# Block counts ahead of the gates, and twelve small matmuls on constants in four short waits of TensorE, in the routing of a mixture-of-experts step

## The chip, the cores and the metric

The kernel runs on one core of one Trainium2 chip. Its time is the device time of one execution in microseconds. It is written by hand in the Bass language: every engine (TensorE or PE, VectorE or DVE, ScalarE or ACT, GpSimd or POOL, and SyncE or SP, which issues most DMAs) has its own program, run in the order in which it is written, and the programs wait for each other on semaphores.

## The reference, cut to what matters

One layer of a decoder on 288 tokens (256 prompt positions and 8 x 4 sample positions) of width 1024, all in float32. First two token-mixing branches and a projection, then a mixture of 32 experts, of which each token uses four:

```python
logits = x2 @ w_router + b_router
top_vals, top_idx = lax.top_k(logits, TOP_K)          # 4 of 32
gates = jax.nn.softmax(top_vals, axis=-1)
...
gu = xb @ w_up[e] + b_up[e]                            # 1024 -> 2048
gate, up = jnp.minimum(gu[:, :F], 7), jnp.clip(gu[:, F:], -7, 7)
act = (up + 1.0) * (gate * jax.nn.sigmoid(1.702 * gate))
out = act @ w_down[e] + b_down[e]                      # 1024 -> 1024
y[token] += out * gate_of_that_token
```

An expert's up weights are 8 MB and its down weights 4 MB, so the 32 experts bring in 384 MB.

## The kernel before

**Stages.** The mixing branches take the first part of the span. Then comes the routing stage (about 350 to 376 us), which this change touches, and then the loop over blocks. A block is up to 32 tokens of one expert. Here 52 blocks come out of the 32 experts; an expert with more than 32 tokens has two.

**Ring of weights.** A buffer `ring` has twelve slots of 1 MB. Slots 0 to 7 hold the up weights of one expert, slots 8 to 11 its down weights. SyncE loads expert 0 while the mixing stage ends (`load_slot(0, k)`). For every further expert it loads slot k as soon as TensorE has used slot k for the last block of the expert before, which it knows from `items_before` (the index of that last block) and the counters `up_used` and `down_used`. In the kernel before, this loop over experts begins with `sp.wait_ge(items_known, 1)`, line 378.

**Routing.** TensorE computes the logits of three token tiles (line 1172 for the two prompt tiles, 1199 for the sample tile), VectorE picks the top four in `route` (lines 817 to 823), giving a 0/1 `mask`. Matmuls with triangular and all-one matrices on the mask give each token its rank within its expert (lines 1204 to 1211) and the counts of tokens of each expert (lines 1214 and 1215, semaphore `counted`). With the ranks, TensorE gathers the tokens of block 0 (`gather_prompt`, `gather_sample`, lines 997 and 1004), ScalarE copies them (`take_rows`), TensorE transposes them (`turn_rows(0)`, line 969) and VectorE scales them into `xT` (`take_x(0)`, line 695). Only then can TensorE start `up(0)` to `up(7)`, the eight up steps of block 0: eight matmul instructions each on one slot (line 1229). The rest of block 0 (its bias, activation and down steps) belongs to body 0 of the loop.

**VectorE in the routing stage, in this order:** the ranks, `take_x(0)`, the gates (exponentials times mask, sum, reciprocal, product: lines 859 to 862), `comb` (the gates at their places in the block, line 866), then the block counts: eight comparisons of the counts with 32, 64, ... (line 872), their sum (874), plus one (875), a running sum over experts in five doublings (878 and 879), and from it the list of blocks (882 to 889, semaphore `listed`), `items_before` and `n_bodies` (890, 891). TensorE turns the list into a row (line 969, semaphore `list_turned`), VectorE copies it to `items` (line 893, semaphore `items_known`). Then VectorE reads a register from `items` and writes `sel` for the gather of block 1 (`select`, line 678, semaphore `sel_ready`).

**TensorE between the ups of block 0:** after `up(4)` it turns the gates (line 1275, waits for `gates_kept`), after `up(6)` it multiplies them with the down biases (`combine(0)`, line 1018), and after `up(7)` it turns the list.

**One body of the loop on TensorE:** gather block i+1 (997, 1004), transpose the raw result of block i (969), `combine_before`, transpose the gathered rows, then `up(0)` to `up(7)` of block i+1 with the four `down` steps of block i (line 1239) between them. A body without waits for weights takes 16.04 us. The ups of body 0 are those of block 1, which is expert 1's first.

**ScalarE** computes the exponentials (line 577), then issues five DMAs of the last norm's weights (lines 578 and 581), and then copies the gathered rows of block 0 (line 587).

Of the kernel before, what the change touches and what calls it, by code (L numbers as in the profile page):

```python
# [22 lines left out]
ALU = mybir.AluOpType  # L23
ACT = mybir.ActivationFunctionType
AX = mybir.AxisListType

P = 128
# [6 lines left out]
NT = 3  # L34
# [49 lines left out]
def hybrid_layer(nc, a, out):  # L84

    with ExitStack() as ctx:
# [154 lines left out]
        rank_ready, gT_ready, items_known = sem("rank_ready"), sem("gT_ready"), sem("items_known")  # L241

# [79 lines left out]
        def _(sp):  # L322
# [55 lines left out]
            sp.wait_ge(items_known, 1)  # L378
# [251 lines left out]
        def _(dve):  # L630
# [195 lines left out]
            def select_first(tt):  # L826
# [30 lines left out]
            take_x(0)  # L857
            dve.wait_ge(exped, 1)
            link(V.tensor_tensor(gates[:], gates[:], mask[:], ALU.mult))
            link(V.tensor_reduce(ss[:, 12:12 + NT], gates[:], AX.X, ALU.add))  # L860
            link(V.reciprocal(ss[:, 12:12 + NT], ss[:, 12:12 + NT]))
            V.tensor_tensor(gates[:], gates[:], ss[:, 12:12 + NT].unsqueeze(2).to_broadcast([P, NT, NE]), ALU.mult
                            ).then_inc(gates_kept, 1)
            dve.wait_ge(gates_kept, 1)
            for tt in range(NT):
                ins = V.tensor_scalar(comb[:, tt], slot_ids[:, 0:BLK].unsqueeze(1).to_broadcast([P, QN, BLK]),
                                      rankm[:, tt, 0:1], gates[:, tt, 0:1], ALU.is_equal, ALU.mult)
            ins.then_inc(comb_ready, 1)

            dve.wait_ge(counted, 1)  # L870
            for r in range(1, MAX_ROUNDS):
                ins = V.tensor_scalar(need[:, r - 1, :], DN[:, 0:NE], float(BLK * r), None, ALU.is_gt)
            link(ins)
# [3 lines left out]
            while step_by < NE:  # L877
                V.tensor_copy(dst[:, 0:step_by], src[:, 0:step_by])
                link(V.tensor_tensor(dst[:, step_by:NE], src[:, step_by:NE], src[:, 0:NE - step_by], ALU.add))
                src, dst, step_by = dst, src, 2 * step_by  # L880

# [8 lines left out]
            V.tensor_scalar(items_before[:], src[0:1, :], 1.0, None, ALU.subtract)  # L890
            V.tensor_scalar(n_bodies[:], src[0:1, NE - 1:NE], 1.0, None, ALU.subtract)
            dve.wait_ge(list_turned, 1)
            V.tensor_copy(items[:], DN[0:1, 0:P]).then_inc(items_known, 1)  # L893
            dve.wait_ge(items_known, 1)
# [69 lines left out]
        def _(pe):  # L964
# [12 lines left out]
            for c in range(KC):  # L977
                for tt in range(NT):
                    r = ROWS[tt]
                    ins = tr(bank[c][:, tt * P:tt * P + r], stage[0:r, tt, c * P:(c + 1) * P])  # L980
                ins.then_inc(x_transposed, 1)

# [213 lines left out]
            sum_quarters(bank[0][:, 256:257])  # L1196
            pe.wait_ge(h2T_ready, 5)
# [4 lines left out]

            pe.wait_ge(routed, 2)
# [18 lines left out]
            gather_sample()  # L1222
            turn_rows(0)

# [43 lines left out]
            for k in range(UP_SLOTS):  # L1268
                up(k, 16 * (FILLS + 1))
                if k == 4:  # L1270
                    pe.wait_ge(gates_kept, 1)
                    for tt in range(NT):
                        r = ROWS[tt]
                        for q in range(QN):
                            ins = mm(TB[q * NE:(q + 1) * NE, tt * P:tt * P + r], gates[0:r, tt, :], ident[0:r, 0:r],
                                     start=True, stop=True)
                    ins.then_inc(gT_ready, 1)
                if k == 6:
                    pe.wait_ge(bdown_in, 16 * QN)
                    pe.wait_ge(combT_ready, 1)  # L1280
                    combine(0, row_out[0])
            pe.wait_ge(listed, 1)
            tr(DN[0:1, 0:P], item_column).then_inc(list_turned, 1)
# [69 lines left out]
```

## Time and profile before

| | |
|---|---|
| median of 3 runs | 1378.38 us (1377.78 to 1382.91) |
| the profiled execution, its time | 1379.41 us |
| its span in the trace | 1377.6 us |
| PE busy / DVE busy / ACT busy / POOL busy | 1193.3 / 516.4 / 255.4 / 67.6 us |
| mean granted clock of TensorE, share of 2.4 GHz | 0.95 |
| read from memory | 447 MB, 326 GB/s over the span |
| chain that ended last | PE 62%, DMA 22%, DVE 7% |

The span starts with the first instruction on record; the 1.8 us between the span and the execution's own time lie outside it. Times in the rows below are counted from the span's start. "L1229" is line 1229 of the kernel, and x64 is a count of instructions. A float32 matmul stands in the trace as two instructions. PEld is the loading of the stationary operand, which may lie beside a matmul. A name ending in q (SPq, ACTq) is an engine's queue issuing DMAs. The granted clock of a stretch is given as a share of 2.4 GHz: 1.00 is that, 0.50 is 1.2 GHz, and a value between means that both levels occur in the stretch.

### The profile page before, as it was taken

The page shows a single profiled execution, that of the slowest core. Times are in us where ns is not written, and L with a number is a line of the kernel's source. Part 1 is how long each engine was busy: PE and PEld are TensorE (multiplying, and loading weights), DVE is VectorE, ACT ScalarE, POOL GpSimd, SP SyncE. Part 2 cuts the span into 40 slices and gives each one's busy share as a digit, 9 for nine tenths or more (in the row PEclk, how much of TensorE's full clock was granted, in tenths as well). Part 3 has the DMA queues.
Part 4 walks back from the last instruction along what each step waited for, and adds up shares of the span by engine and source line. Part 5 has one row for each costly group of instructions (what it writes and reads, how often), then busy time and mean ns, then how long its engine had stood idle before and what let it go on. Part 6 is the DMA issues. An engine that isn't in the chain of part 4 may idle for free.

```text
span 1377.6 us, 28967 instructions
## 1 busy us (share of the span) xinstructions
PE 1193.3 (87%) x11107; PEld 582.5 (42%) x11108; DVE 516.4 (37%) x1236; ACT 255.4 (19%) x497; POOL 67.6 (5%) x69
## 2 busy tenths in 40 slices
PE   5889999999889997887689669868799798689996
PEld 3667777775434342333233224313234243234333
DVE  0789961221433333323133223313233233133334
ACT  3001122200212221211112112212122122122222
POOL 0293210000000000000000000000000000000000
PEclk9999999999799999999899999999899899899999
DMA  9962333331497799999999999999999999999992
GB/s 260 317 203 93 130 117 113 111 128 59 152 402 320 299 393 416 419 417 418 418 405 394 417 418 396 420 418 418 417 414 395 417 396 420 418 418 395 393 393 88
DMA packets 110946, 448.91 MB, mean 326 GB/s; under 512 B 8526, under 2 KB 42894, under 8 KB 78107
## 3 DMA queue, kind: packets, MB, share of 16 engines
q1 hardware_dynamic: 110190, 446.57, 81.8%
q10 hardware_dynamic: 685, 1.17, 0.3%
q0 software_dynamic: 48, 0.85, 0.2%
q8 instruction: 15, 0.25, 0.1%
q14 instruction: 8, 0.07, 0.0%
HBM read 447.00 MB, written 2.42 MB: 326 GB/s over the span
## 4 chain that ended last, share of the span: by engine, by line
PE 62%; DMA 22%; DVE 7%; SPq 3%; POOL 3%; issue 3%; ACT 0%; POOLq 0%; DVEq 0%
PE banks L1229 22%; DMA ring<-in_w_up 22%; PE banks L1036 12%; PE banks L1239 10%; PE banks L1018 4%; PE banks L969 4%; DVE R L710 4%; PE banks L997 3%; SPq L373 3%; PE banks L1148 2%; POOL big L433 2%; PE banks L1004 2%; PE banks L1027 2%; DVE big L695 1%; POOL prod L455 1%
## 5 line engine op out<-in xcount | busy, mean ns | idle before, releaser
L1229 PE MATMUL banks<-ring,big 128*32 128x512 f32 x3328 | 448.8, 630 | 126.0 <-DMA ring<-in_w_up 113.2
L304 DVE TENSOR_TENSOR xt<-xt,banks 128x1024 f32<-128x1024 f32 x106 | 129.1, 1219 | 499.5 <-PE banks L1018 499.5
L1239 PE MATMUL banks<-ring,R 128*32 128x256 f32 x3328 | 223.8, 388 | 1.2 <-DVE R L919 1.2
L1229 PEld LDWEIGHTS banks<-ring,big 128*32 128x32 f32 x3328 | 95.2, 112 | 279.1 <-DMA ring<-in_w_up 172.4
L1036 PE MATMUL banks<-hT,ring 128*128 128x288 f32 x768 | 195.6, 417 | 7.9 <-ACT stage L483 5.9
L1239 PEld LDWEIGHTS banks<-ring,R 128*32 128x32 f32 x3328 | 113.5, 113 | 168.0 <-issue 134.8
L1036 PEld LDWEIGHTS banks<-hT,ring 128*128 128x128 f32 x768 | 149.6, 196 | 50.1 <-ACT stage L483 6.3
L602 ACT COPY R<-banks 128x256 f32<-128x256 f32 x52 | 19.3, 372 | 517.8 <-PE banks L1239 517.8
L710 DVE SCALAR_TENSOR_TENSOR R<-big,convw,R 128x256 f32<-128x256 f32 x240 | 99.3, 494 | 0.0
L906 DVE TENSOR_TENSOR big<-banks,bupT 128x512 f32<-128x512 f32 x52 | 36.0, 692 | 138.2 <-PE banks L969 138.2
L1018 PE MATMUL banks<-R 32*128 32x256 f32 x848 | 77.0, 434 | 0.7 <-ACT R L602 0.7
L997 PE MATMUL banks<-stage,R 128*32 128x256 f32 x832 | 57.3, 394 | 18.8 <-issue 15.6
L610 ACT ACT_TABLE_LOAD x51 | 65.4, 1283 | 5.4 <-DVE items L893 4.5
L1036 PE MATMUL banks<-R,ring 128*128 128x288 f32 x256 | 62.3, 407 | 0.0
L1018 PEld LDWEIGHTS banks<-R 32*128 32x128 f32 x848 | 34.1, 187 | 57.7 <-issue 57.7
L969 PE MATMUL banks<-ident,big 128*128 128x128 f32 x312 | 57.4, 294 | 1.2 <-ACT big L592 0.7
L997 PEld LDWEIGHTS banks<-stage,R 128*32 128x32 f32 x832 | 22.9, 111 | 74.3 <-issue 63.1
L1036 PEld LDWEIGHTS banks<-R,ring 128*128 128x128 f32 x256 | 48.7, 190 | 13.2
L592 ACT COPY big<-banks 128x512 f32<-128x512 f32 x52 | 30.4, 585 | 120.1 <-PE banks L1229 120.1
L969 PEld LDWEIGHTS banks<-ident,big 128*128 128x128 f32 x312 | 32.5, 141 | 45.4 <-issue 42.4
L687 DVE TENSOR_SCALAR R<-slot_ids,R 128x128 f32 x153 | 43.6, 342 | 0.0
L433 POOL TENSOR_TENSOR big<-stage,tmpc 128x256 f32<-128x256 f32 x8 | 38.8, 4851 | 60.0 <-DVE WT L669 44.0
(217 smaller groups left out, 680.3 us busy)
## 6 DMA issues: line engine op xcount, KB each, us to landing
ring<-in_w_up SPq DMA_DIRECT2D x256, 1024.0 KB, 11.1
ring<-in_w_down SPq DMA_DIRECT2D x128, 1024.0 KB, 9.6
ring<-in_w_in SPq DMA_DIRECT2D x24, 1024.0 KB, 10.1
ring<-in_w_branch_b SPq DMA_DIRECT2D x4, 1024.0 KB, 5.0
ring<-in_w_branch_a SPq DMA_DIRECT2D x4, 1024.0 KB, 4.9
ring<-in_w_out SPq DMA_DIRECT2D x4, 1024.0 KB, 5.0
xt<-in_x_prompt SPq DMA_DIRECT2D x2, 512.0 KB, 3.9
out_y_prompt<-xt SPq DMA_DIRECT2D x2, 512.0 KB, 2.7
```

The costliest lines, as they stand in the source:

```text
L304: nc.vector.tensor_tensor(dst, dst, rows, ALU.add).then_inc(y_added, 1)
L373: sp.dma_start(dst, src).then_inc(slot_full[k], 16)
L433: nc.gpsimd.tensor_tensor(cprompt[:, c, HIST:HIST + SEQ], tmpv[:, c % 2, 0:SEQ], tmpc[:, c % 2, 0:SEQ], ALU.mult)
L610: nc.scalar.activation(ss[:, 15:16], eps_col[:], ACT.Sigmoid)
L687: ins = V.tensor_scalar(comb[:, tt], slot_ids[:, bass.ds(rank0, BLK)].unsqueeze(1).to_broadcast([P, QN, BLK]), rankm[:, tt, bass.ds(expert ...
L710: ins = V.scalar_tensor_tensor(acc, cprompt[:, c, k:k + SEQ], convw[:, c, k:k + 1], acc, ALU.mult, ALU.add)
L969: return nc.tensor.transpose(dst, src, ident[0:n, 0:n])
L997: mm(XB[q * BLK:(q + 1) * BLK, 0:256], sel[:, tt, :], stage[:, tt, q * 256:(q + 1) * 256], start=tt == 0, stop=False)
L1018: ins = mm(rows[:, q, :], combT[q * BLK:(q + 1) * BLK, tt * P:(tt + 1) * P], out_sb[q * BLK:(q + 1) * BLK, :], start=True, stop=True)
L1036: ins = mm(dst[:, 0:T], w[:, k, h * P:(h + 1) * P], src[:, k, :], start=k == 0, stop=k == KC - 1)
L1229: ins = mm(UP[g * BLK:(g + 1) * BLK, :], xT[:, k, :], ring[:, k, g * 512:(g + 1) * 512], start=k == 0, stop=k == UP_SLOTS - 1)
L1239: ins = mm(DN[q * BLK:(q + 1) * BLK, 0:256], actT[:, f % 4, f // 4, :], ring[:, UP_SLOTS + j, h * D + q * 256:h * D + (q + 1) * 256], star ...
```

## The change

VectorE works out the block counts and `items_before` first, before `take_x(0)` and the gates; the eight comparisons become one instruction over 8 x 32 elements. A new semaphore `before_known` tells SyncE that `items_before` is there, and SyncE's loop over experts waits for that in place of `items_known`. The list of blocks follows `take_x(0)`, then the gates, then the copy of the turned list, then `comb`. On TensorE the list is turned after `up(3)` in place of after `up(7)`, the gates after `up(5)` in place of `up(4)`, and `combine(0)` comes after `up(7)`. A function `keep_busy(n)` issues n matmuls of the constant matrices `ones` (128 x 128) and `below` (128 x 32 of it) into a bank that nobody reads then; `keep_busy(3)` stands at four places: before the logits of the sample tile, before the rank matmuls, between the gather of block 0 and its transposition, and between this and `up(0)`.

```diff
--- before.py
+++ after.py
@@ -239,6 +239,7 @@
         logits_ready, shifted, exped, routed, first_selected = (
             sem(n) for n in ("logits_ready", "shifted", "exped", "routed", "first_selected"))
         rank_ready, gT_ready, items_known = sem("rank_ready"), sem("gT_ready"), sem("items_known")
+        before_known = sem("before_known")
 
         sel_ready, gathered, rows_ready = sem("sel_ready"), sem("gathered"), sem("rows_ready")
         rows_turned, xT_ready = sem("rows_turned"), sem("xT_ready")
@@ -375,7 +376,7 @@
             for k in range(SLOTS):
                 sp.wait_ge(*mix_block_used(MIX_BLOCKS - SLOTS + k))
                 load_slot(0, k)
-            sp.wait_ge(items_known, 1)
+            sp.wait_ge(before_known, 1)
             with sp.Fori(1, NE) as e:
                 before = sp.value_load(items_before[0:1, bass.ds(e - 1, 1)], min_val=0, max_val=MAX_ITEMS)
                 for k in range(UP_SLOTS):
@@ -854,23 +855,10 @@
             select_first(2)
             V.tensor_tensor(gates[:], lx[:, :, 0:NE], top8[:, :, 0:1].to_broadcast([P, NT, NE]), ALU.subtract
                             ).then_inc(shifted, 1)
-            take_x(0)
-            dve.wait_ge(exped, 1)
-            link(V.tensor_tensor(gates[:], gates[:], mask[:], ALU.mult))
-            link(V.tensor_reduce(ss[:, 12:12 + NT], gates[:], AX.X, ALU.add))
-            link(V.reciprocal(ss[:, 12:12 + NT], ss[:, 12:12 + NT]))
-            V.tensor_tensor(gates[:], gates[:], ss[:, 12:12 + NT].unsqueeze(2).to_broadcast([P, NT, NE]), ALU.mult
-                            ).then_inc(gates_kept, 1)
-            dve.wait_ge(gates_kept, 1)
-            for tt in range(NT):
-                ins = V.tensor_scalar(comb[:, tt], slot_ids[:, 0:BLK].unsqueeze(1).to_broadcast([P, QN, BLK]),
-                                      rankm[:, tt, 0:1], gates[:, tt, 0:1], ALU.is_equal, ALU.mult)
-            ins.then_inc(comb_ready, 1)
-
             dve.wait_ge(counted, 1)
-            for r in range(1, MAX_ROUNDS):
-                ins = V.tensor_scalar(need[:, r - 1, :], DN[:, 0:NE], float(BLK * r), None, ALU.is_gt)
-            link(ins)
+            link(V.tensor_tensor(need, DN[:, 0:NE].unsqueeze(1).to_broadcast([P, MAX_ROUNDS - 1, NE]),
+                                 slot_ids[:, BLK:MAX_ROUNDS * BLK:BLK].unsqueeze(2).to_broadcast([P, MAX_ROUNDS - 1, NE]),
+                                 ALU.is_gt))
             link(V.tensor_reduce(ends_a, need.rearrange("p r e -> p e r"), AX.X, ALU.add))
             link(V.tensor_scalar(ends_a, ends_a, 1.0, None, ALU.add))
             src, dst, step_by = ends_a, ends_b, 1
@@ -878,6 +866,9 @@
                 V.tensor_copy(dst[:, 0:step_by], src[:, 0:step_by])
                 link(V.tensor_tensor(dst[:, step_by:NE], src[:, step_by:NE], src[:, 0:NE - step_by], ALU.add))
                 src, dst, step_by = dst, src, 2 * step_by
+            V.tensor_scalar(items_before[:], src[0:1, :], 1.0, None, ALU.subtract).then_inc(before_known, 1)
+            V.tensor_scalar(n_bodies[:], src[0:1, NE - 1:NE], 1.0, None, ALU.subtract)
+            take_x(0)
 
             link(V.tensor_scalar(started, src, item_ids[:, 0:1], None, ALU.is_le))
             V.tensor_reduce(item_expert, started, AX.X, ALU.add)
@@ -887,10 +878,20 @@
             link(V.tensor_tensor(item_column, item_column, item_expert, ALU.add))
             link(V.tensor_scalar(item_expert, item_ids[:, 0:1], src[:, NE - 1:NE], None, ALU.is_lt))
             V.tensor_tensor(item_column, item_column, item_expert, ALU.mult).then_inc(listed, 1)
-            V.tensor_scalar(items_before[:], src[0:1, :], 1.0, None, ALU.subtract)
-            V.tensor_scalar(n_bodies[:], src[0:1, NE - 1:NE], 1.0, None, ALU.subtract)
+
+            dve.wait_ge(exped, 1)
+            link(V.tensor_tensor(gates[:], gates[:], mask[:], ALU.mult))
+            link(V.tensor_reduce(ss[:, 12:12 + NT], gates[:], AX.X, ALU.add))
+            link(V.reciprocal(ss[:, 12:12 + NT], ss[:, 12:12 + NT]))
+            V.tensor_tensor(gates[:], gates[:], ss[:, 12:12 + NT].unsqueeze(2).to_broadcast([P, NT, NE]), ALU.mult
+                            ).then_inc(gates_kept, 1)
             dve.wait_ge(list_turned, 1)
             V.tensor_copy(items[:], DN[0:1, 0:P]).then_inc(items_known, 1)
+            dve.wait_ge(gates_kept, 1)
+            for tt in range(NT):
+                ins = V.tensor_scalar(comb[:, tt], slot_ids[:, 0:BLK].unsqueeze(1).to_broadcast([P, QN, BLK]),
+                                      rankm[:, tt, 0:1], gates[:, tt, 0:1], ALU.is_equal, ALU.mult)
+            ins.then_inc(comb_ready, 1)
             dve.wait_ge(items_known, 1)
             select(dve.value_load(items[0:1, 1:2], min_val=0, max_val=COLUMN_MAX))
             dve.wait_ge(combined, 1)
@@ -979,6 +980,11 @@
                     r = ROWS[tt]
                     ins = tr(bank[c][:, tt * P:tt * P + r], stage[0:r, tt, c * P:(c + 1) * P])
                 ins.then_inc(x_transposed, 1)
+
+            def keep_busy(n):
+
+                for _ in range(n):
+                    mm(TB[:, 0:NE], ones[:], below[:, 0:NE], start=True, stop=True)
 
             def sum_quarters(dst):
 
@@ -1194,12 +1200,14 @@
             ins.then_inc(x2_transposed, 1)
             pe.wait_ge(quarters_squared, 1)
             sum_quarters(bank[0][:, 256:257])
+            keep_busy(3)
             pe.wait_ge(h2T_ready, 5)
             for k in range(KC):
                 ins = mm(bank[5][0:NS, 0:NE], hT[:, k, SEQ:T], wr[:, k, :],
                          start=k == 0, stop=k == KC - 1)
             ins.then_inc(logits_ready, 1)
 
+            keep_busy(3)
             pe.wait_ge(routed, 2)
             mm(bank[7][:, 0:NE], below[:], mask[:, 0, :], start=True, stop=True)
             mm(bank[7][:, NE:2 * NE], ones[:], mask[:, 0, :], start=True, stop=False)
@@ -1220,7 +1228,9 @@
             pe.wait_ge(first_selected, 3)
             pe.wait_ge(rows_kept, 3)
             gather_sample()
+            keep_busy(3)
             turn_rows(0)
+            keep_busy(3)
 
             def up(k, fills):
 
@@ -1267,7 +1277,10 @@
             pe.wait_ge(xT_ready, 1)
             for k in range(UP_SLOTS):
                 up(k, 16 * (FILLS + 1))
-                if k == 4:
+                if k == 3:
+                    pe.wait_ge(listed, 1)
+                    tr(DN[0:1, 0:P], item_column).then_inc(list_turned, 1)
+                if k == 5:
                     pe.wait_ge(gates_kept, 1)
                     for tt in range(NT):
                         r = ROWS[tt]
@@ -1275,12 +1288,9 @@
                             ins = mm(TB[q * NE:(q + 1) * NE, tt * P:tt * P + r], gates[0:r, tt, :], ident[0:r, 0:r],
                                      start=True, stop=True)
                     ins.then_inc(gT_ready, 1)
-                if k == 6:
-                    pe.wait_ge(bdown_in, 16 * QN)
-                    pe.wait_ge(combT_ready, 1)
-                    combine(0, row_out[0])
-            pe.wait_ge(listed, 1)
-            tr(DN[0:1, 0:P], item_column).then_inc(list_turned, 1)
+            pe.wait_ge(bdown_in, 16 * QN)
+            pe.wait_ge(combT_ready, 1)
+            combine(0, row_out[0])
             pe.wait_ge(items_known, 1)
             bodies = pe.value_load(n_bodies[0:1, 0:1], min_val=NE - 1, max_val=MAX_ITEMS - 1)
             with pe.Fori(0, bodies) as i:
```

## Rows read from the trace of the kernel before

**Rows 1.** The page of the profile, its first line.
```profile
span 1377.6 us, 28967 instructions
```

**Rows 2.** Waits of the SyncE queue: us in total, times, longest us.
```profile
...
SPq L373 <- PE banks L1239: 393.0, 124, 13.1
...
SPq L379 <- DVE items L893: 22.0, 1, 22.0
```

**Rows 3.** Chain that ended last, 340 to 520 us: start, us, what.
```profile
...
374.43 0.29 DVE items L893
...
376.35 0.37 SPq L373
...
380.58 19.42 DMA ring<-in_w_up
400.05 1.06 PE banks L1229 x8
...
402.03 1.07 PE banks L997 x16
...
406.57 1.92 PE banks L1229 x16
...
418.08 1.07 PE banks L997 x16
```

**Rows 4.** Timeline, TensorE, 350 to 384 us: start, us, what, [idle before <- releaser].
```profile
...
350.37 1.97 PE L1172 MATMUL banks<-wr,hT 128*128 128x32 f32 x16
...
353.11 0.81 PE L1199 MATMUL banks<-wr,hT 128*32 128x32 f32 x16 [0.40 <-DVE hT L842]
...
354.44 0.64 PE L1204 MATMUL banks<-R,below 128*128 128x32 f32 x2 [0.52 <-DVE R L823]
...
359.42 1.94 PE L997 MATMUL banks<-stage,R 128*32 128x256 f32 x16
...
362.85 0.69 PE L969 MATMUL banks<-ident,big 128*128 128x128 f32 x2 [0.49 <-ACT big L587]
...
364.06 6.01 PE L1229 MATMUL banks<-ring,big 128*32 128x512 f32 x40 [0.52 <-DVE big L695]
...
374.12 0.27 PE L969 MATMUL banks<-ident,R 128*1 128x128 f32 x1
...
377.28 1.87 PE L997 MATMUL banks<-stage,R 128*32 128x256 f32 x16 [2.88 <-DVE R L678]
...
383.36 1.92 PE L1229 MATMUL banks<-ring,big 128*32 128x512 f32 x16 [0.31 <-DVE big L695]
```

**Rows 5.** Windows by granted clock, core 0: busy time of each engine in each.
```profile
...
352.80:353.60 0.80, 0.49 (x14) 0.49 (x15) 0.73 (x4) 0.21 (x1) 0.00 (x0) 0.94 1.02 420
...
354.40:359.40 5.00, 4.96 (x20) 4.63 (x20) 2.43 (x14) 2.07 (x3) 0.00 (x0) 0.50 1.03 419
359.40:364.00 4.60, 3.65 (x27) 1.08 (x26) 0.42 (x2) 0.37 (x1) 0.00 (x0) 0.50 1.01 396
364.00:367.20 3.20, 3.14 (x16) 0.80 (x20) 3.02 (x17) 0.00 (x0) 0.00 (x0) 0.51 0.05 12
367.20:374.50 7.30, 7.19 (x85) 2.19 (x77) 3.19 (x23) 0.40 (x1) 0.00 (x0) 1.00 0.00 0
...
377.40:380.80 3.40, 3.40 (x28) 1.39 (x25) 0.28 (x1) 0.60 (x2) 0.00 (x0) 0.50 0.88 337
```

**Rows 6.** Timeline, VectorE and the ScalarE queue, 358 to 384 us.
```profile
...
359.04 1.86 ACTq L581 DMA_DIRECT2D R<-in_norm_final_g  x4
...
365.76 0.87 DVE L872 TENSOR_SCALAR R<-banks 128x32 f32<-128x32 f32 x8
...
368.96 0.24 DVE L882 TENSOR_SCALAR R<-R,item_ids 128x32 f32<-128x32 f32 x1
...
376.03 0.53 DVE L678 TENSOR_SCALAR R<-slot_ids,R 128x32 f32 x3 [1.32 <-issue]
...
383.23 0.42 DVE L916 TENSOR_TENSOR big<-big 128x256 f32<-128x256 f32 x1
```


## The prediction, made before the changed kernel was run

> **What bounds the kernel now.** I read the waits of the SyncE queue first, because the change moves one of them. SyncE waits for TensorE's use of slots in nearly all its waits (393.0 us for the downs alone); the one exception in the middle is a single wait of 22.0 us for `items` [rows 2]. The chain of waits then says whether that wait matters. It does: the copy of the list at 374.43 us releases SyncE's first issue at 376.35, from there the chain lies in the transfers of expert 1's up weights for 19.42 us, and the eighth up step of body 0 can start only at 400.05 [rows 3]. The windows show that the DMA engines had next to nothing to do from 364.0 to 374.5 (shares 0.05 and 0.00) [rows 5]. So a piece of the critical path is "list known, then load", in front of idle DMA engines. Behind 400 us the loop runs on pairs of "TensorE frees a slot, the slot is loaded, TensorE goes on". All of these waits are relative, so what is won at 400 us is kept to the end of the 1377.6 us span [rows 1] if TensorE and the DMAs both come earlier.
>
> The timeline of TensorE shows what else stands ahead of body 0: four short waits of 0.40, 0.52, 0.49 and 0.52 us, a first up step at 364.06, the turned list at 374.12, then 2.88 us of waiting for `sel`, a gather at 377.28 and the first up step of body 0 at 383.36 [rows 4]. The windows show the clock: upper level until about 353.6, 1.2 GHz from there to 367.2, although TensorE had matmuls in flight for 4.96 of 5.00 us after 354.4, and again 1.2 GHz from 377.4 to 380.8 [rows 5].
>
> **The fillers.** `keep_busy(3)` is six instructions, each with a 128-column stationary operand and 32 columns moved, the form of lines 1172 and 1204 to 1214. At the upper clock 16 of these took 1.97 us, 0.12 each [rows 4], so six take 0.7. At the lower, 20 lie between 354.44 and 359.42 [rows 4], 0.25 each; two of their gaps are waits, so I take 1.4 for six, with 1.5 as upper bound. The first filler runs at the upper clock: 0.7 - 0.4 = 0.3 late. The other three, at the lower clock, cost 1.4 less the wait that they fill: 0.9 each. Sum: the ranks start 1.2 late, `up(0)` 3.0 late, at 367.1. Bounds: with the upper clock throughout four fillers cost 0.3 + 3 x 0.2 = 0.9; nothing excludes that the clock is held, so that case is a rival.
>
> **Does the clock stay up?** The rows speak against it. Before 353.6 TensorE had been busy with nothing but such small matmuls, waited 0.40 us, and lost the upper clock; then 20 of the same form, without a gap worth naming, did not bring it back; the 512-column matmuls of the ups did, after 3.1 us [rows 4, 5]. A filler adds more of the form that neither held nor restored the clock. The Trainium skill ("TensorE: Matmul & The Clock Gate", section "Why this matters for your kernels") asks for TensorE to be kept busy and free of long idle gaps to get and keep the full clock. By that rule the fillers would hold it, and the sum would be that of the first rival below; the 4.96 busy us at half clock are a case that the rule doesn't cover.
>
> **The counts.** `counted` is set at 359.42, with the delay at 360.7. VectorE then needs one 128 x 256 comparison; the nearest row of that size is 0.42, bounds 0.22 (a fraction of it) and 0.87 (the eight that it replaces), both harmless. The rest of the chain up to line 882 took 368.96 - 365.76 - 0.87 = 2.33 us [rows 6], and with `items_before` and `n_bodies`, two small ones, it ends at 363.8. `take_x(0)` now stands behind that; its input comes at 363.54 + 2.1 = 365.6, so the counts are hidden with 1.8 us to spare. SyncE needs 376.35 - 374.72 = 1.6 us from the semaphore to its first issue [rows 3]: it could issue at 365.4. But slot 0 is free only when `up(0)` is through. At 1.2 GHz an up takes 1.7 us (twice the 0.86 that eight of the 16 instructions at 406.57 take), so the first issue is at 367.1 + 1.8 = 368.9. The wait on the list turns into the wait on `up_used`.
>
> **From the first issue to the eighth slot.** Before: 400.05 - 376.35 = 23.7 us [rows 3]. The engines were idle before, as they are now: the other transfers end at 364.0 [rows 5]. So the DMAs allow the eighth up at 368.9 + 23.7 = 392.6. The freeing of the other slots, one per 0.86 to 1.7 us, is faster than the loading.
>
> **TensorE's own way there.** From `up(0)` to the turned list was 374.12 - 364.06 = 10.1 us with 3.1 at the lower clock; the same work plus the list's 0.2 ahead of its end: 367.1 + 10.3 = 377.4. The wait for `sel`, 2.88 us, goes: the list is turned after `up(3)`, at about 372.3 (two ups at 1.7, two at 0.86), and copied 0.29 later [rows 3]; `comb` (three instructions of 128 x 128, at most the 0.42 of a 128 x 256 each), VectorE's register read (1.32) and `select` (0.53) [rows 6] end by 375.8. Behind `take_x(0)` stand the list (eight small instructions, at most the 0.24 of line 882 each, done by 368.0) and now behind it the gates (four instructions of 96 elements, about 1.1, done by 369.2, wanted after `up(5)`, past 373). ScalarE's copy of the weights lies beside `up(6)` and `up(7)`. What remains is TensorE's own register reads, 0.2 to 0.9 us (its step from the eighth up into the next gather was 402.03 - 401.11 = 0.9 in body 0, [rows 3]); I take 0.5: gather at 377.9. From gather to `up(0)` of the body was 6.1 us with the clock down [rows 4], and is 406.57 - 402.03 = 4.5 with it up [rows 3]. TensorE has not idled, so 4.5: `up(0)` at 382.4. From there to the next body's gather is 418.08 - 406.57 = 11.5 us when no slot is late: 393.9. By the DMAs it is 392.6 + 1.98 = 394.6, in place of 402.03.
>
> **The sum.** 402.03 less 393.9 to 394.6 is 7.4 to 8.1 us; where the clock falls a little later than in this execution (a bare 0.4 us filler and some rank matmuls at 0.12) a few tenths come on top. I take 7.9. The profiled execution took 1379.41, 1.0 over the median of 1378.38, within the 5 us spread of the three; measured from the median: 1370.5.
>
> **Rivals.** *The clock is held throughout.* Then the fillers cost 0.9 and the rest is faster: 14 rank and count instructions at 0.12 follow the sample tile's mask, which comes at 355.9 as now, to 357.6, and the gather takes half of its 2.9 us: 359.1. Now ScalarE is late: its five DMA issues, which end at 359.04 + 1.86 = 360.9 [rows 6] and would end at 360.2, stand ahead of the copy. `take_x(0)` ends at 361.8, the first issue is at 362.9, the eighth slot at 386.6: 13.4 us won, 1365.0. For it: the waits are the only gaps; against: the 4.96 us above.
>
> *The clock falls only after the first ranks.* Then the second filler and ten rank instructions run at 0.12, and `up(0)` is about 2.6 us earlier than I forecast: 10.3 won, 1368.1. For it: the fall at 353.6 came just ahead of that stretch.
>
> *The clock comes back late.* It came back 3.1 us into the ups [rows 5]; the ups now start at another moment. If all eight ups run at 1.2 GHz (5.8 more of them at 0.86 us extra) `sel` and the body are up to 5 us later: 2 to 4 us won, 1375, no change that shows. For it: the fillers push the dense matmuls 3.0 us back.
>
> *Slower, same mechanism further:* the clock stays at 1.2 GHz through body 0 too. Then the eight ups (13.8) and the small work between them (3.0) end at 383.9, the body's own `up(0)` comes at 390.5, and its ups and downs take 20.5 in place of 10.25 us: the eighth at 411 in place of 400.05, 1389. It decides only if the lower clock lasts past 390, where the gain is used up; against it, dense matmuls brought the clock back after 3.1 us at 364 and after 3.4 at 377.4 [rows 5].
>
> *The earlier issue is worth nothing because TensorE is the bound* is no rival of its own: TensorE's own arrival (393.9) is in the sum, and equals the DMAs' (394.6).
>
> **How the numbers follow.** Forecast 0.52, clock held 0.12, falls later 0.17, comes back late 0.14, slower 0.05. A measurement of this kernel tells about 0.5%, 6.9 us, from no change. The forecast's own range is 1368 to 1373; a quarter of it lies above 1371.5. Faster: 0.39 + 0.12 + 0.17 = 0.68; same: 0.13 + 0.14 = 0.27; slower 0.05. The range takes in the held clock and most of the late one: 1364.0 to 1375.5.
>
> **What the changed profile would show.** SyncE's first issue at about 369 us, waiting for line 1229 and not for VectorE; no wait for `sel` ahead of body 0; its gather near 378, its eighth up near 392.7; `keep_busy` instructions at 0.2 to 0.25 us each in the three later places, with a granted clock of 0.50 from the ranks to the ups. If they show 0.12 each and 1.00, the first rival holds. The forecast is wrong if the DMAs' first issue waits for something else, or if the gain at 402 is not there at 1350, which would mean that the loop has slack that I have not seen.

## The result

The changed kernel took 1369.62 us (median of 6, 1368.18 to 1373.62) beside 1379.15 for the kernel before on the same chip (6, 1377.78 to 1384.16): ratio 0.9926, 95% interval 0.9904 to 0.9948, 9.5 us faster. The prediction was 1370.5 us, range 1364.0 to 1375.5, "faster" with a chance of 0.68. The profiled execution took 1368.47 us, its span is 1366.7. Medians and ratios below leave out two single executions, of 2919 and 6448 us.

**The wait of SyncE.** Waits of the SyncE queue after the change: us in total, times, longest us.

```profile
...
SPq L374 <- PE banks L1239: 301.8, 152, 23.7
...
SPq L380 <- DVE items_before L869: 9.8, 1, 9.8
```

The wait of 22.0 us on `items` [rows 2] is one of 9.8 us on `items_before`, and behind it SyncE waits for the ups (L1239).

**The routing stage.** Timeline of the changed kernel: start, us, what. L987 is `keep_busy`, L1003 the gather, L970 a transposition, L1239 the ups; "second logits" below is the last row of L1178, the logits of the second prompt tile. A time with a plus is counted from their start.

```profile
...
351.24 1.97 PE L1178 MATMUL banks<-wr,hT 128*128 128x32 f32 x16
...
353.44 0.83 PE L987 MATMUL banks<-below,ones 128*128 128x32 f32 x6
...
354.20 0.69 PE L1206 MATMUL banks<-wr,hT 128*32 128x32 f32 x16
...
354.83 0.85 PE L987 MATMUL banks<-below,ones 128*128 128x32 f32 x6
...
355.52 0.39 PE L1212 MATMUL banks<-R,below 128*128 128x32 f32 x2
...
360.29 1.94 PE L1003 MATMUL banks<-stage,R 128*32 128x256 f32 x16
...
363.12 0.85 PE L987 MATMUL banks<-below,ones 128*128 128x32 f32 x6
363.15 0.17 DVE L869 TENSOR_SCALAR items_before<-R 1x32 int32<-1x32 f32 x1
...
364.06 0.75 PE L987 MATMUL banks<-below,ones 128*128 128x32 f32 x6
364.26 0.42 DVE L696 TENSOR_TENSOR big<-banks,cols 128x256 f32<-128x256 f32 x1 [0.89 <-PE banks L970]
...
364.74 3.64 PE L1239 MATMUL banks<-ring,big 128*32 128x512 f32 x32
...
366.01 7.44 SPq L374 DMA_DIRECT2D ring<-in_w_up  x8
...
368.31 0.27 PE L970 MATMUL banks<-ident,R 128*1 128x128 f32 x1
...
374.23 1.07 PE L1003 MATMUL banks<-stage,R 128*32 128x256 f32 x16 [0.67 <-issue]
...
378.79 1.50 PE L1239 MATMUL banks<-ring,big 128*32 128x512 f32 x12 [0.30 <-DVE big L696]
```

This answers to [rows 4]. All of it lies 0.87 us later than before (the second logits start at 351.24, not 350.37), because the mixing stage ended later in this execution. From the second logits on, up(0) starts at +13.50 us (before +13.69) and the first issue for expert 1 at +14.77 (before +25.98). `items_before` is written at 363.32, and SyncE's 1.6 us from there would allow an issue at 364.9; it comes at 366.01, 1.27 after the start of `up(0)`: the step that releases it is now `up(0)`. The 2.88 us of waiting for `sel` are gone, and body 0's gather starts 9.49 us after `up(0)` in place of 13.22.

**The end of the stretch.** Chain of waits of the changed kernel, for [rows 3]:

```profile
...
373.12 16.55 DMA ring<-in_w_up
389.71 1.07 PE banks L1239 x8
...
391.74 1.07 PE banks L1003 x16
```

The eighth up of body 0 starts at 389.71 in place of 400.05. From the first issue it is 23.70 us, before it was 23.70. It still ends a wait for the transfers (16.55 us of the chain), but a short one for TensorE: 0.6 us. So this trace wins 11.2 us between the second logits and the eighth up, less the 0.9 us that came in ahead of them.

**The clock.** Windows of the changed kernel, columns as in [rows 5]:

```profile
...
351.20:356.20 5.00, 5.00 (x58) 4.88 (x54) 2.81 (x15) 1.60 (x5) 0.00 (x0) 1.00 0.77 260
356.60:360.30 3.70, 3.54 (x16) 3.29 (x16) 1.21 (x7) 0.85 (x2) 0.00 (x0) 0.50 1.02 416
360.30:363.00 2.70, 2.70 (x25) 0.78 (x24) 2.36 (x13) 0.00 (x0) 0.00 (x0) 0.50 1.03 411
363.10:364.70 1.60, 1.60 (x18) 1.58 (x14) 0.68 (x5) 0.37 (x1) 0.00 (x0) 1.00 0.99 388
364.70:374.20 9.50, 8.87 (x99) 2.80 (x98) 4.35 (x20) 2.36 (x4) 0.00 (x0) 1.00 0.77 301
```

Here the clock fell at about 356.2 and came back at about 363.0, ahead of the ups. All four fillers ran at the upper clock, at 0.75 to 0.85 us each. The signs that the prediction named for itself (first issue near 369 us, eighth up near 392.7, the last three fillers at 1.2 GHz) are not there: they came at 366.0 and 389.7, and the fillers' clock was 1.00. Of its first rival only half is there, since the clock did fall between them. The experiments say what it means.

### The profile page after: what moved, and what is told of

It is laid out like the page before. It is cut to its first block, busy times and chain, and to the rows that moved or that the text cites. A ratio compares the mean times of both kernels' runs of the same rounds, so it can differ in the third digit from the quotient of the medians.

```text
span 1366.7 us, 29008 instructions
## 1 busy us (share of the span) xinstructions
PE 1192.6 (87%) x11131; PEld 583.7 (43%) x11132; DVE 516.6 (38%) x1229; ACT 255.6 (19%) x497; POOL 54.6 (4%) x69
## 4 chain that ended last, share of the span: by engine, by line
PE 61%; DMA 22%; DVE 9%; SPq 3%; issue 3%; POOL 2%; ACT 0%; POOLq 0%; DVEq 0%
PE banks L1239 22%; DMA ring<-in_w_up 22%; PE banks L1042 11%; PE banks L1249 10%; DVE R L711 6%; PE banks L1024 4%; PE banks L970 4%; PE banks L1003 3%; SPq L374 2%; PE banks L1154 2%; PE banks L1010 2%; PE banks L1033 2%; DVE big L696 1%; POOL prod L456 1%; POOL big L434 1%
## 5 line engine op out<-in xcount | busy, mean ns | idle before, releaser
L1239 PE MATMUL banks<-ring,big 128*32 128x512 f32 x3328 | 448.8, 630 | 118.0 <-DMA ring<-in_w_up 105.9
L1239 PEld LDWEIGHTS banks<-ring,big 128*32 128x32 f32 x3328 | 96.0, 112 | 267.5 <-DMA ring<-in_w_up 160.4
L1042 PE MATMUL banks<-hT,ring 128*128 128x288 f32 x768 | 192.4, 412 | 2.8 <-DVE WT L670 1.4
L1003 PE MATMUL banks<-stage,R 128*32 128x256 f32 x832 | 56.5, 389 | 15.7 <-issue 15.2
L970 PE MATMUL banks<-ident,big 128*128 128x128 f32 x312 | 56.9, 291 | 0.7 <-ACT big L593 0.7
L1042 PEld LDWEIGHTS banks<-R,ring 128*128 128x128 f32 x256 | 48.6, 190 | 13.4
L1003 PEld LDWEIGHTS banks<-stage,R 128*32 128x32 f32 x832 | 22.6, 110 | 71.2 <-issue 62.9
L970 PEld LDWEIGHTS banks<-ident,big 128*128 128x128 f32 x312 | 32.3, 140 | 43.6 <-issue 42.0
L970 PE MATMUL banks<-ident,R 128*128 128x128 f32 (+4 forms) x205 | 34.4, 263 | 2.7 <-DVE big L658 2.7
```

What stands on the lines that cost most here:

```text
L970: return nc.tensor.transpose(dst, src, ident[0:n, 0:n])
L1003: mm(XB[q * BLK:(q + 1) * BLK, 0:256], sel[:, tt, :], stage[:, tt, q * 256:(q + 1) * 256], start=tt == 0, stop=False)
L1042: ins = mm(dst[:, 0:T], w[:, k, h * P:(h + 1) * P], src[:, k, :], start=k == 0, stop=k == KC - 1)
L1239: ins = mm(UP[g * BLK:(g + 1) * BLK, :], xT[:, k, :], ring[:, k, g * 512:(g + 1) * 512], start=k == 0, stop=k == UP_SLOTS - 1)
```

## The experiments

Times are medians of 5 to 12 executions, each compared with the kernel before on its own chip, whose medians there were 1379.5 (first four), 1379.8 (next four) and 1380.0 us (last four). A ratio's interval is 0.0013 to 0.0023 to either side. Differences between two runs are taken from their ratios where they ran on different chips.

**1. Counts only.** The changed kernel without the fillers.

```diff
-            keep_busy(3)
```
(at all four places)

> The changed kernel without its twelve fillers: all four keep_busy(3) taken out, the order of VectorE, SyncE and TensorE as changed. Theory A (the gain is the earlier first issue of expert 1's loads; the fillers are neither gain nor loss beyond the moment at which the clock changes): up(0) at about 364 us as in the kernel before, first issue 365.9, eighth slot 23.7 later at 389.6: 10.4 us under the kernel before, about 1368.7, within 1.5 us of the changed kernel. Theory B (the fillers hold the upper clock past the first ranks and bring it back ahead of the ups): 2.5 us or more slower than the changed kernel, 1372 or above, with 1.2 GHz from about 353.6 to 367.

Measured: 1370.34 us, ratio 0.9925 [0.9909, 0.9942]; the changed kernel has 0.9926. The fillers are no part of the gain. In its trace, without a single filler, the clock fell 5.8 us behind the start of the second logits, later than in the changed kernel (4.9) and than before (3.1). So the later fall needs no filler. Theory B, which wanted 1372 us or more, falls.

**2. Fillers only.** The kernel before with `keep_busy(3)` at the four places.

> The kernel before with the four keep_busy(3) at their places and nothing else changed. Theory A: within 1.5 us of the kernel before (1379), since each filler at the upper clock costs 0.75 to 0.85 us in a wait of 0.4 to 0.5, and the list's path is the same. If the clock is down under the last three, up to 3 us slower. Theory B: 1 to 3 us faster than before, 1376 to 1378, with the clock up until about 356.5 and again before the ups.

Measured: 1382.62 us, ratio 1.0019 [1.0005, 1.0032]: some 2.6 us slower. TensorE's timeline in this kernel:

```profile
...
352.58 0.83 PE L986 MATMUL banks<-below,ones 128*128 128x32 f32 x6
...
354.34 1.49 PE L986 MATMUL banks<-below,ones 128*128 128x32 f32 x6
...
363.31 0.96 PE L986 MATMUL banks<-below,ones 128*128 128x32 f32 x6
...
364.35 0.75 PE L986 MATMUL banks<-below,ones 128*128 128x32 f32 x6
```

The clock fell near 353.3, 2.9 us behind the start of the second logits, as early as without fillers, and the second filler took 1.49 us. But the traced execution is the fastest of the twelve (1377.94), and its eighth up comes 0.5 us earlier than before, counted from the second logits. So the loss rests on the medians alone; where it arises no trace shows.

**3. SyncE waits for the list again.** All of the change but its wait.

```diff
-            sp.wait_ge(before_known, 1)
+            sp.wait_ge(items_known, 1)
```

> The changed kernel, but SyncE waits for items_known again as in the kernel before. The list is known at 368.9 in the changed kernel. Theory A (the first issue sets the eighth up step of body 0): first issue at 368.9 + 1.6 = 370.5, 4.5 us later than the 366.0 of the changed kernel, eighth slot at 394.2, time 1374.1. Rival (TensorE's own earlier arrival after the list is turned earlier is what gives the gain): within 1.5 us of the changed kernel, 1369.6.

Measured: 1375.42 us, ratio 0.9963 [0.9948, 0.9978]: about half of the gain is gone. Waits of the SyncE queue in this kernel:

```profile
...
SPq L374 <- PE banks L1239: 300.2, 144, 23.7
...
SPq L380 <- DVE items L889: 19.0, 1, 19.0
```

SyncE waits 19.0 us for the list and has eight waits fewer for the ups (144, not 152): the eight first issues find their slots free. The first issue is at 373.21, the eighth up 23.79 us later. It came 2.7 us later than I expected; in this trace the clock stayed down until 5.4 us into the ups, and the list is turned behind `up(3)`.

**4. TensorE's old order.** Counts only, and besides the list turned behind `up(7)`, the gates behind `up(4)`, `combine(0)` behind `up(6)`, as before.

> The counts run without fillers and with TensorE's order of the kernel before (list turned after up(7), gates after up(4), combine(0) after up(6)); VectorE's order and SyncE's earlier wait as changed. If TensorE's own arrival at the eighth up of body 0 counts beside the transfers: first issue still at 365.9 (transfers allow 389.6), but body 0 starts at 377.3 as before and its eighth up comes at 393.6 without a wait for weights: about 3.5 us slower than with the new order, 1373. If the transfers alone set it: no difference from the counts run, 1370.

Measured: 1373.43 us, ratio 0.9948 [0.9929, 0.9967], 3.1 us over counts only by the medians (forecast 3.5). Timeline of this kernel (L1235 the ups):

```profile
...
367.71 6.88 PE L1235 MATMUL banks<-ring,big 128*32 128x512 f32 x40 [0.52 <-DVE big L696]
...
369.85 9.40 SPq L374 DMA_DIRECT2D ring<-in_w_up  x8
...
381.76 1.07 PE L1003 MATMUL banks<-stage,R 128*32 128x256 f32 x16 [2.84 <-DVE R L679]
...
398.02 1.07 PE L1235 MATMUL banks<-ring,big 128*32 128x512 f32 x8
```

The first issue is as early as in the counts run (2.14 us after `up(0)`), but the 2.84 us of waiting for `sel` are back, and the eighth up starts 28.2 us after the first issue with no wait for a slot. Here TensorE is the bound. About 1.5 us of its delay is the clock: it fell again at 382.8, behind the wait for `sel`, and gather to `up(0)` of body 0 took 6.0 us in place of 4.6. All four traces with TensorE's old order lost the clock again within body 0, ahead of its eighth up (at 377.4, 377.2, 382.8 and 384.3 us); none of the ten with the new order did. So the gain has two parts, and each is worth something alone: the early issue with the old order gives 0.52%, the new order with the old wait 0.37%, both together 0.75%, which is less than their sum of 0.89%.

One variant was not run: the wait alone, with nothing reordered. In the kernel before, VectorE had written `items_before` 4.0 us ahead of `items`:

```profile
...
370.56 0.16 DVE L890 TENSOR_SCALAR items_before<-R 1x32 int32<-1x32 f32 x1
```

By the 1.6 us from semaphore to issue, the first issue could have come at about 372.3 in place of 376.35. That is an estimate; how much of the gain comes without VectorE's new order stays open.

**5. Wide fillers.** The changed kernel with one matmul of 256 columns for three of 32.

```diff
-                    mm(TB[:, 0:NE], ones[:], below[:, 0:NE], start=True, stop=True)
+                    mm(TB[:, 0:256], ones[:], slot_ids[:, 0:256], start=True, stop=True)
```
(with `keep_busy(1)` for `keep_busy(3)`)

> The changed kernel with each keep_busy(3) of 32 columns replaced by one matmul of 256 columns on constants (two instructions, about 0.43 us together at the upper clock), at the same four places. Theory A (small matmuls do not hold the clock, dense ones may): if the clock stays up from 353 to the ups, up(0) comes at most 1.5 us earlier, where ScalarE's five DMA issues (to about 361.8) are the next limit: 1368. If it falls all the same: within 1 us of the changed kernel. Theory B (the small ones already do all that fillers can): no difference in clock and time.

Measured: 1368.60 us, ratio 0.9917 [0.9901, 0.9934]. Windows of this kernel:

```profile
...
351.90:359.40 7.50, 6.90 (x64) 5.91 (x60) 4.35 (x23) 2.60 (x6) 0.00 (x0) 1.00 0.83 311
359.40:363.00 3.60, 3.22 (x32) 1.38 (x31) 3.13 (x17) 0.62 (x2) 0.00 (x0) 1.00 1.03 414
363.00:372.50 9.50, 8.82 (x97) 2.80 (x97) 4.36 (x20) 2.36 (x4) 0.00 (x0) 1.00 1.01 392
```

In this trace the clock did not fall at all ahead of the eighth up, the only one of fourteen. `up(0)` is 11.1 us behind the second logits, and the eighth up 35.8 in place of 38.5: what "the clock is held" is worth here is 2.6 us. Against the kernel before that is 13.8 us on this stretch, near the 13.4 of the prediction's first rival. The median (0.9917 beside 0.9926) doesn't tell the run from the changed kernel.

**6. Wide fillers in the kernel before.**

> The kernel before with the four wide fillers (one matmul of 256 columns each) and nothing else. In the changed kernel the same fillers kept the clock up from 353 through the ups. If they do so here, the list is known about 1.5 to 3 us earlier (up(0) at about 361.5 to 362.5, the eight ups all at the upper clock) and the time is 1376 to 1377.5. If the clock falls all the same: 1379 to 1380.

Measured: 1377.39 us, ratio 0.9982 [0.9968, 0.9996]; about 2.5 us faster. The clock fell all the same, 6.8 us behind the second logits, came back 0.2 us into the ups, and fell again at 384.3, 0.8 us behind the end of a 2.48 us wait for a transfer.

**7. Fillers doubled.** `keep_busy(6)` in the changed kernel.

> The changed kernel with keep_busy(6) in place of keep_busy(3): 24 small matmuls in the same four waits. Theory A (fillers are only work on the way to up(0)): the waits are already full, so each of the four adds its six instructions whole, 0.7 us at the upper clock and 1.3 to 1.5 at the lower: up(0) and the first issue 2.8 to 5 us later, 1372.5 to 1374.5. Theory B (they hold the clock): the upper clock throughout the routing stage in the profile, and no more than 1 us slower.

Measured: 1377.35 us, ratio 0.9977 [0.9961, 0.9993], some 7 us slower than the changed kernel, more than the 3 to 5 that I expected. TensorE's timeline in it:

```profile
...
354.71 1.50 PE L987 MATMUL banks<-below,ones 128*128 128x32 f32 x12
...
356.77 1.53 PE L987 MATMUL banks<-below,ones 128*128 128x32 f32 x12
...
365.43 1.53 PE L987 MATMUL banks<-below,ones 128*128 128x32 f32 x12
...
367.04 1.42 PE L987 MATMUL banks<-below,ones 128*128 128x32 f32 x12
368.39 2.51 PE L1239 MATMUL banks<-ring,big 128*32 128x512 f32 x12
```

Twelve instructions take 1.42 to 1.53 us in each of the four places, at the upper clock for nearly all of them. `up(0)` is 15.9 us behind the second logits, 2.4 more than in the changed kernel; and the clock, up from 365.3, fell again at 368.7, behind 24 more small instructions and the transposition, 0.3 us into the ups, so that the next 3.4 us of them ran at 1.2 GHz. The traced execution (1373.1) is again one of the fastest of its twelve. Its eighth up is at +41.9, 3.4 us behind that of the changed kernel's first trace and 0.6 behind that of its second (below). The rest of the 7 us is in no trace.

**8. The norm's weights issued later.** Wide fillers, and ScalarE's five DMA issues moved from the routing stage to behind the loop.

> The changed kernel with wide fillers, and ScalarE's five DMA issues of the last norm's weights moved from the routing stage to behind the loop, so that they no longer stand ahead of its copy of the gathered rows. In the wide run the copy started 0.6 us after the gather's end because of them. Expected: up(0) and first issue 0.5 us earlier, 1368.1. If the issues behind the loop are late for the last norm: 1 to 3 us slower at the end.

Measured: 1367.72 us, ratio 0.9912 [0.9889, 0.9935]. The 0.5 us earlier `up(0)` that I expected did not come: it is at +13.5, with number 5 at +11.1. Whether the moved issues did anything can't be told from it: in this trace the clock was down under the gather, which ended late enough for ScalarE to be free in either order.

**9 to 12. The same again on one chip,** the changed kernel, counts only, number 8, and number 8 with wide fillers only in the first two waits.

> The changed kernel a second time, for a second trace of it and a comparison on one chip with the next ones. If the moment at which the clock falls and comes back is set by the kernel (theory B), the second trace has it 5.2 us after the start of the second logits and back 1.7 us ahead of up(0), as the first. If it is not (theory A), they lie elsewhere, in the 3.2 to 6.8 us and -1.7 to +5.3 us that the traces so far show. Time 1369 to 1371.

> The counts run (no fillers) a second time. Theory A: within 1 us of the changed kernel on the same chip, clock moments anywhere in the same ranges. Theory B: slower by 2 us or more.

> Wide fillers and the norm's weights issued behind the loop, a second time, beside the changed kernel on the same chip: 1 to 2.5 us faster than it if wide fillers put off the fall of the clock, none if the first result was chance.

> As the run before, but wide fillers only in the first two waits, none beside the transposition of the gathered rows. If the last two fillers only delay up(0): 0 to 1 us faster than with four. If they bring the upper clock back ahead of the ups: 1 us or more slower, with the clock coming back 2 to 5 us after up(0).

Measured: changed kernel 1371.22 (0.9934 [0.9915, 0.9953]), counts only 1370.86 (0.9930 [0.9911, 0.9949]), number 8 again 1366.49 (0.9904 [0.9885, 0.9924]), two wide fillers 1369.56 (0.9927 [0.9910, 0.9945]). The changed kernel and counts only agree within 0.4 us, as they did the first time.

Number 8 had the lowest median both times it ran, here 4.7 us under the changed kernel; all five of its executions lie below all six of that kernel's (1368.78 the slowest, 1368.82 the fastest). In the two traces the spans differ by 6.0 us, but 2.9 of that lies ahead of the second logits, in a stage where the programs are alike, 2.7 between them and the eighth up, and 0.4 behind. So what is due to the wide fillers is less than the medians say.

With only the first two wide fillers the median is 3.1 us over number 8's. The clock fell later than in number 8 (8.4 us behind the second logits, not 6.4 and 6.6) and came back 3.8 us into the ups, not 0.1 to 0.3 ahead of them. Yet its eighth up is at +37.9, 0.6 us sooner than number 8's +38.5; what makes this trace the longer one again lies ahead of the second logits, which start 3.1 us later. That the last two fillers are worth the 3.1 us is not shown.

The second trace of the changed kernel is the telling one. Its timeline:

```profile
...
353.59 1.97 PE L1178 MATMUL banks<-wr,hT 128*128 128x32 f32 x16
...
357.18 0.86 PE L987 MATMUL banks<-below,ones 128*128 128x32 f32 x6
...
365.52 1.49 PE L987 MATMUL banks<-below,ones 128*128 128x32 f32 x6
...
367.28 1.33 PE L987 MATMUL banks<-below,ones 128*128 128x32 f32 x6
...
368.54 2.79 PE L1239 MATMUL banks<-ring,big 128*32 128x512 f32 x12
...
370.67 0.37 SPq L374 DMA_DIRECT2D ring<-in_w_up  x1
```

and its windows:

```profile
...
353.60:358.20 4.60, 4.60 (x55) 4.52 (x52) 2.49 (x12) 1.26 (x4) 0.00 (x0) 1.00 0.74 245
358.70:367.50 8.80, 8.53 (x49) 6.06 (x50) 4.13 (x23) 1.47 (x3) 0.00 (x0) 0.50 1.01 401
...
368.50:371.90 3.40, 3.40 (x17) 0.79 (x20) 1.74 (x9) 0.00 (x0) 0.00 (x0) 0.50 0.17 19
372.20:382.00 9.80, 9.13 (x113) 3.13 (x105) 2.80 (x8) 2.73 (x5) 0.00 (x0) 1.00 0.96 394
```

The program is the same, the clock is not: it fell again 4.8 us behind the second logits, but came back only at about 372, 3.5 us into the ups, where in the first trace it came back 1.7 us ahead of them. The last two fillers took 1.49 and 1.33 us, `up(0)` is at +14.95 and the first issue at +17.08. Counts only, with the clock down over the same stretch (from 359.0 to 372.6), has

```profile
...
354.05 1.97 PE L1178 MATMUL banks<-wr,hT 128*128 128x32 f32 x16
...
367.74 3.64 PE L1235 MATMUL banks<-ring,big 128*32 128x512 f32 x16 [0.52 <-DVE big L696]
...
369.88 0.37 SPq L374 DMA_DIRECT2D ring<-in_w_up  x1
```

that is `up(0)` at +13.69 and the issue at +15.83. In this pair the fillers cost 1.3 us of TensorE's way, and bring nothing ahead of the ups.

**All traces together.** The time from the second logits to the eighth up of body 0, and from there to the end of the span:

```
                              clock falls   back, from   up(0)   issue   eighth up   rest of
                              after logits  up(0)                                     the span
before                        +3.1          +3.1         +13.7   +26.0   +49.7       977.5
fillers only                  +2.9          -1.5         +14.7   +25.4   +49.2       976.7
wide fillers only             +6.8          +0.2         +13.4   +24.3   +48.2       977.1
changed                       +4.9          -1.7         +13.5   +14.8   +38.5       977.0
changed, second trace         +4.8          +3.5         +15.0   +17.1   +41.2       976.7
counts only                   +5.8          +2.6         +13.5   +15.6   +39.4       977.0
counts only, second trace     +4.9          +4.9         +13.7   +15.8   +40.4       976.8
SyncE waits for the list      +6.2          +5.4         +14.5   +22.9   +46.7       976.6
old order of TensorE          +4.9          +4.9         +13.7   +15.8   +44.0       976.6
fillers doubled               +6.0          -3.1         +15.9   +17.7   +41.9       976.9
wide fillers                  never         -            +11.1   +12.4   +35.8       977.4
number 8                      +6.4          -0.3         +13.5   +14.7   +38.5       976.3
number 8, second trace        +6.6          -0.1         +13.5   +14.8   +38.5       976.2
number 8, two wide fillers    +8.4          +3.8         +11.4   +13.5   +37.9       976.3
```

The clock columns give the first fall and the first return; with the fillers doubled it fell once more, 0.4 us into the ups, until 3.7 us into them. The expectations give 5.2 and 3.2 us for falls that finer windows put at 4.9 and 3.1.

The last column settles the step on which everything else rested: whatever happens ahead of the eighth up, 976.2 to 977.5 us follow it in all fourteen traces. The loop has no slack that would eat an earlier start. The three lowest values are those of the three traces with the norm's weights issued late; whether that edit is the reason is not shown.

## Why the prediction was right, step by step

**The wait that bounds.** Right. "List known, then load" was on the path: number 3 puts that wait back, and the eighth up comes 5.5 to 8.2 us later than in the changed kernel's traces. Number 4 shows the other bound, TensorE's own way. The wait on the list did turn into the wait on `up(0)`: the issue follows its start by 1.3 to 2.1 us (forecast 1.8), and `items_before` comes 1.1 us earlier than it would have to.

**23.7 us from the first issue to the eighth slot.** Right to the tenth in the changed kernel (23.70), 23.5 to 24.5 in the others where the transfers are the bound or nearly so.

**TensorE's own way.** The wait for `sel` went (0.67 us of TensorE's own issue are left, taken as 0.5), and gather to `up(0)` of body 0 took 4.56 (taken as 4.5). That TensorE and the transfers would arrive together was right within 0.6 us.

**The counts ahead of `take_x(0)`.** The one 128 x 256 comparison took 0.42 us, and VectorE waited 0.89 us for the gathered rows afterwards, so the counts were covered. The forecast had 1.8 us to spare; in the second trace, with the clock down, VectorE waited 1.79 us.

**The fillers.** This is the term that was mis-sized, by the clock it assumed and not by the price. I put up(0) 3.0 us later, with three fillers at 1.2 GHz. The price at that clock was right (1.3 to 1.5 us, taken as 1.4; at the upper 0.75 to 0.86, taken as 0.7), but in both traces the second filler and the first ranks ran at the upper clock, and in one of them the last two also: up(0) came 0.2 us earlier than before in the first trace and 1.3 later in the second. The trace that I had of before is one of the two with the earliest fall of all fourteen (3.1 us behind the second logits; the other is fillers only, 2.9). In the first trace 11.2 us are won from the second logits on, near the 10.3 of the rival "falls only after the first ranks"; in the second 8.5, near the 7.4 to 8.1 of the forecast. The measured 9.5 us lies between, so 1370.5 was right partly since it stands between two cases, one of which I had at 0.17. And it was luck in one more way: the gain was forecast 1.6 us too small (7.9), but counted from a median of three executions, 1378.38, that lay 0.8 us under that of six. Nor do the 9.5 us measure this stretch alone: the second logits start anywhere from 350.2 to 354.1 us in the fourteen traces.

**"Nothing but such small matmuls."** This reading of the clock's fall in the kernel before holds only for the 3.1 us from the second logits on; until 350.4 us TensorE ran matmuls of 256 columns (L1156).

**The rivals.** *The clock is held throughout* did not come about by the fillers of this change. The Trainium skill ("TensorE: Matmul & The Clock Gate", section "Why this matters for your kernels") asks for a busy TensorE without long gaps. The trace does not agree: in the changed kernel TensorE was busy for 5.00 of 5.00 us, nearly all of it with small matmuls, directly ahead of the fall at 356.2. With the wide fillers of number 5 the clock stayed up in its one trace; with the same four fillers it fell in number 6 and in both traces of number 8. *The clock comes back late* is what number 3 and the second counts trace show (5.4 and 4.9 us into the ups); between the two counts traces it is worth 1.0 us (39.4 and 40.4 to the eighth up), not the whole gain. *Slower* was not seen: body 0 ran at the upper clock from start to end in every trace of the changed kernel.

**What stays open.** What decides at which moment the clock falls and comes back within these ranges: the same program did it differently twice, so nothing in the code alone. Open too is the loss with fillers only (2.6 us), and with doubled fillers what goes beyond the 0.6 to 3.4 us of its trace: both lie in executions without one. And the wait moved without a new order was not run.

## What to carry to other kernels

Give a queue that only issues transfers the one number that it needs as soon as that is known, not the last product of the chain that contains it; then look for what is late next, here a slot still in use, and move the consumer's own waits along with it: here the early issue alone gave about two thirds of the gain and the consumer's new order alone about half. Before a filler goes into a wait, take its duration at the lower clock, less the wait, as its price: twelve small matmuls in waits of 0.4 to 0.5 us bought nothing with the counts moved, and cost 0.2% (interval 0.05 to 0.32%) without. Compare stages by their distance from a common event, not from the span's start: here the stage ahead varied by 3.8 us between traces of kernels that are alike in it, more than the 2.6 us that the held clock is worth.

## What was not expected of the hardware

The same program had its clock back 1.7 us ahead of `up(0)` in one execution and 3.5 us behind it in another. The clock fell behind small matmuls (128-column stationary operand, 32 columns moved) even when TensorE had been busy without a gap: at 356.2 us in the changed kernel, and at 368.7 with doubled fillers, where it had only just come back. At 1.2 GHz six of them took 1.33 to 1.49 us, at 2.4 GHz 0.75 to 0.86.
